# Attention: one half gate chunk of each unit moves from ahead of the first turn of the probabilities to behind the last one

## The chip, the cores and the metric

One core of a Trainium2 chip runs the whole program. The metric is device time in microseconds (us), as the median of several executions. The profile comes from one more execution. The engines are called PE (TensorE matmuls), PEld (TensorE weight loads), DVE (VectorE), ACT (ScalarE), POOL (GpSimd) and SP (SyncE, which only issues DMAs here).

## The reference, cut to what matters

The program computes two blocks, one after the other. The second block has two layers, and each begins with a projection, sliding window attention with 16 meta tokens, and a convolution branch. What matters here is, for each layer:

```
u = h @ w_in[i]                      # q, k, v, conv inputs and two gates come out of one projection
s = q k^T * scale + bias             # per block of 128 queries: keys = 16 meta, 128 previous, 128 own
m = max(max(s), sink); p = exp(s - m); p = p / (sum(p) + exp(sink - m))
o = p_meta @ v_meta + p_band @ v_band
mix = (sigmoid(gate_a) * (o @ w_attn_proj) + sigmoid(gate_c) * y_conv) @ w_out
```

There are 8 query heads in 2 groups of 4 that share keys and values, and 512 tokens behind the 16 meta tokens. All is float32.

## The kernel before, in words

`project_and_attend` (L2351) does the projection and the attention of one layer. It is called once for each of the two layers. Its work on TensorE has two kinds.

The first kind is the projection. A *half chunk* is 128 output channels for 264 of the 528 token columns: 8 products over k, each of which the trace counts as 2 instructions (for float32 every matmul here is 2 instructions, the turns excepted). The accumulators are 2 PSUM banks, `ring`. ACT copies a bank out (`take`, L2560), and the half chunk after the next one needs that copy (`taken`, L2462). The last 32 half chunks are those of the gates (`gate`, L2470). They are needed only by the next stage, so 16 of them are kept for the attention, where they fill TensorE's time between the dependent steps. There they are issued in *parts*, each of 4 of the 8 products (8 instructions in the trace). The diff moves such parts: "a half gate chunk" in the title is such a part, half of a half chunk.

The second kind is the attention, in units. A unit is one block of queries with one group of heads. Layer 0 has 10 units: two for the meta queries, with one block of keys, two with two blocks of keys (the first real block has no previous one), and six with three. Layer 1 has 8: two with two blocks, six with three. For unit u the steps are:

- `scores(u + 1)` on TensorE (L2484), one unit ahead;
- `turn(u, m)` on TensorE (L2500), one for each block m of keys: four transposes of the probabilities into the PSUM bank `ptr`. The turn of m = 0 waits for `scaled` of the unit (POOL, L2456). Each turn waits for `t_out` of the one before, since there is one bank;
- the move of `ptr` to `pt` on ACT (L2624), one for each turn, which raises `t_out`;
- `weigh_values(u)` on TensorE (L2510), the products with the values, which waits for the last `t_out`.

On DVE, behind `scores(u + 1)`: the bias, the maximum, and at the end `maxed` (L2694). On ACT, behind the move of m = 0: `soft(u + 1)` (L2569), four exponentials with sums and a small one, which waits for `maxed`. Then DVE inverts the sum (L2698) and POOL scales the probabilities. ACT closes the unit by copying the result out (L2629, `o_out`). Behind unit `len(units) - 4` ACT also runs four Silus over the convolution's result (L2634).

How many parts a unit gets is set by `upto(u)` (L2409), which spreads the 16 half chunks evenly: in layer 0 the ten units get 2, 4, 2, 4, 4, 2, 4, 2, 4, 4 parts, in layer 1 every unit gets 4. Before the change the unit's parts stand as follows (numbers of parts in brackets, for 3 blocks and 4 parts): scores(u+1), [2], turn 0, [1], turn 1, [1], turn 2, weigh_values(u). With 3 blocks and 2 parts it is scores, turn 0, [1], turn 1, [1], turn 2, weigh_values. ACT has the same order written out: it takes those half chunks that are complete by then, ahead of the move of each turn.

```
stop = last_part - (len(keys) - 1 - m)           # PE, L2549: parts up to here stand ahead of turn m
stop = (last_part - (len(keys) - 1 - m)) // 2    # ACT, L2617: half chunks taken ahead of move m
```

Of the kernel before, what the change touches and what calls it, by code (L numbers as in the profile page):

```python
# [2350 lines left out]
def project_and_attend(core, A, i, weights, mix_in):  # L2351
# [5 lines left out]
    for n in range(TILES):  # L2357
        for hk in range(KVH):
            keys = [(0, META, TILES)] + ([(META + (n - 1) * P, P, n - 1)] if n else []) + [(META + n * P, P, n)]
# [10 lines left out]
    with ExitStack() as ctx:  # L2370
# [38 lines left out]
        def upto(u):  # L2409

            return EARLY + 2 + (GATES - EARLY - 2) * (u + 1) // len(units)

        def slot(j):

            return j % 2 * 2 + j // 2
# [10 lines left out]
        with core.block() as block:  # L2426
# [32 lines left out]
            def _(pe):  # L2459
# [24 lines left out]
                def scores(u):  # L2484
                    hk, nq, q0, keys = units[u]
                    if u:
                        pe.wait_ge(s_read, u)
                    lo, width = keys[-1][0] + keys[-1][1], sum(k[1] for k in keys[1:])
                    for j in range(G):
                        c, b = divmod(j, 2)  # L2490
                        rows = slice(b * HD, (b + 1) * HD)
                        q = core.q_t[rows, hk * 2 + c, q0:q0 + nq]
                        last = pe.matmul(meta(u)[:, b, c, :], q, core.k_t[rows, hk, 0:META], start=True, stop=True)
                        if width:
                            last = pe.matmul(main(u)[:, b, c, 2 * P - width:], q, core.k_t[rows, hk, lo - width:lo], start=True, stop=True)
                    last.then_inc(s_made, 1)
# [3 lines left out]
                def turn(u, m):  # L2500
                    hk, nq, q0, keys = units[u]
                    at, nk = sum(k[1] for k in keys[:m]), keys[m][1]
                    if moves[0]:
                        pe.wait_ge(t_out, moves[0])
                    for j in range(G):
                        last = pe.transpose(ptr[0:nk, j * nq:(j + 1) * nq], s[0:nq, u % 2, slot(j), at:at + nk], ident[0:nq, 0:nq])
                    last.then_inc(t_made, 1)
                    moves[0] += 1

                def weigh_values(u):  # L2510
                    hk, nq, q0, keys = units[u]
                    pe.wait_ge(t_out, moves[0])
                    if u:
                        pe.wait_ge(o_out, u)
                    for m, (k0, nk, vt) in enumerate(keys):
                        for par in range(2):
                            heads = pt[0:nk, m, 0:G * nq].rearrange("p (c r q) -> p c r q", r=2, q=nq)[:, :, par, :]
                            last = pe.matmul(po[par * HD:(par + 1) * HD, 0:2 * nq], core.v_tok[0:nk, vt, hk * HD:(hk + 1) * HD],
                                             heads, start=m == 0, stop=m == len(keys) - 1)
                    last.then_inc(o_made, 1)  # L2520
# [22 lines left out]
                done = 2 * (EARLY + 2)  # L2543
                for u, (hk, nq, q0, keys) in enumerate(units):
                    if u + 1 < len(units):
                        scores(u + 1)
                    last_part = 2 * upto(u)
                    for m in range(len(keys)):
                        stop = last_part - (len(keys) - 1 - m)  # L2549
                        for part in range(done, stop):  # L2550
                            gate(part // 2, part % 2)
                        done = max(done, stop)
                        if m == 0:
                            pe.wait_ge(scaled, u + 1)
                        turn(u, m)
                    weigh_values(u)

            @block.scalar
            def _(act):
                def take(n, dst, f, half):  # L2560
                    act.wait_ge(projected, n + 1)
                    act.activation(dst[:, cols(half)], ring[:, n % RINGS, 0:HALF], f).then_inc(taken, 1)

                def gate(h):
                    if h // 2 >= 2 * DK - CCK - 1:
                        act.wait_ge(normed, CCK)
                    take(gate_half(h), core.gates[:, h // 2, :], ACT.Copy, h % 2)

                def soft(u):  # L2569
                    hk, nq, q0, keys = units[u]  # L2570
                    width = sum(k[1] for k in keys)
                    x = st[0:nq, u % 2]
                    act.wait_ge(maxed, u + 1)
                    for j in range(G):
                        act.activation(s[0:nq, u % 2, j, 0:width], s[0:nq, u % 2, j, 0:width], ACT.Exp,
                                       bias=x[:, 2, j:j + 1], accum_out=x[:, 3, j:j + 1])
                    act.activation(x[:, 1, :], x[:, 1, :], ACT.Exp).then_inc(exped, 1)

                act.wait_ge(padded, 1)
                for n in range(first_gate):  # L2580
                    c, half = divmod(n, 2)
                    if c < 4:
                        take(n, val[:, c, :], ACT.Copy, half)
                    elif c < 8:
                        take(n, glu[:, c - 4, CW - 1:], ACT.Sigmoid, half)
                    elif c < 12:
                        take(n, core.q_t[:, c - 8, :], ACT.Copy, half)
                    else:
                        take(n, core.k_t[:, c - 12, :], ACT.Copy, half)
                act.wait_ge(v_made, 1)  # L2590
                act.activation(core.v_tok[:, 0:4, :].rearrange("p t c -> p (t c)"), ps[:, 0, :], ACT.Copy)
                act.activation(core.v_tok[0:META, 4, :], ps[0:META, 1, 0:P], ACT.Copy).then_inc(v_out, 1)
                for h in range(EARLY):
                    gate(h)
                act.wait_ge(centred, CCK)
                act.wait_ge(taken, SUMS)
                act.sem_inc(taken, 1)
                for c in range(CCK):
                    act.wait_ge(centred, CCK + c + 1)
                    if c == CCK - 1:  # L2600
                        act.wait_ge(taken, SUMS + 1)
                        act.sem_inc(taken, 1)
                    act.activation(sq[:, c, :], core.conv[:, c, :], ACT.Square).then_inc(squared, 1)
                for h in range(EARLY, EARLY + 2):
                    gate(h)
                for half in range(2):
                    n = SQUARES + half
                    act.wait_ge(projected, n + 1)
                    act.activation(rt[:, cols(half)], ring[:, n % RINGS, 0:HALF], ACT.Sqrt, scale=1.0 / CC, bias=eps).then_inc(taken, 1)
                act.wait_ge(taken, SQUARES + 2)  # L2610
                act.sem_inc(rooted, 1)
                soft(0)
                moves, done = 0, EARLY + 2
                for u, (hk, nq, q0, keys) in enumerate(units):
                    last_part = 2 * upto(u)
                    for m, (k0, nk, _) in enumerate(keys):
                        stop = (last_part - (len(keys) - 1 - m)) // 2  # L2617
                        for h in range(done, stop):
                            gate(h)
                        done = max(done, stop)  # L2620
                        act.wait_ge(t_made, moves + 1)
                        if u:
                            act.wait_ge(o_made, u)
                        act.activation(pt[0:nk, m, 0:G * nq], ptr[0:nk, 0:G * nq], ACT.Copy).then_inc(t_out, 1)  # L2624
                        moves += 1
                        if m == 0 and u + 1 < len(units):
                            soft(u + 1)
                    act.wait_ge(o_made, u + 1)
                    act.activation(core.attn[:, hk * 2:hk * 2 + 2, q0:q0 + nq],  # L2629
                                   po[:, 0:2 * nq].rearrange("p (c q) -> p c q", c=2), ACT.Copy).then_inc(o_out, 1)  # L2630
                    if u == len(units) - 4:
                        for c in range(CCK):
                            act.wait_ge(normed, c + 1)
                            act.activation(core.conv[:, c, :], core.conv[:, c, :], ACT.Silu, scale=param(c, 0), bias=param(c, 1)  # L2634
                                           ).then_inc(silu, 1)
# [967 lines left out]
```

## Time and profile before

| | |
|---|---|
| Time, median of 3 runs | 3231.21 us (3228.75 to 3231.43) |
| The profiled execution's own time | 3231.08 us |
| Its span | 3229.2 us |
| TensorE busy (matmuls) | 93% of the span |
| DVE, ACT, POOL busy | 32%, 17%, 7% |
| Attention units of layer 0 | about 1373 to 1492 us |
| Attention units of layer 1 | about 2292 to 2404 us |

A row of the timeline gives start, duration, engine, line, operation, output and inputs, and how many instructions were merged. Behind it, in brackets, stands how long the engine had been idle and what ended that idle time; "issue" means nothing that the profile shows. PE and PEld are the same queue: a load stands ahead of its matmul. Starts of loads are the better clock for TensorE's order, since they show when the queue reached a step.

### The profile page before, as it was taken

The page shows a single profiled execution, that of the slowest core. Times are in us where ns is not written, and L with a number is a line of the kernel's source. Part 1 is how long each engine was busy: PE and PEld are TensorE (multiplying, and loading weights), DVE is VectorE, ACT ScalarE, POOL GpSimd, SP SyncE. Part 2 cuts the span into 40 slices and gives each one's busy share as a digit, 9 for nine tenths or more (in the row PEclk, how much of TensorE's full clock was granted, in tenths as well). Part 3 has the DMA queues.
Part 4 walks back from the last instruction along what each step waited for, and adds up shares of the span by engine and source line. Part 5 has one row for each costly group of instructions (what it writes and reads, how often), then busy time and mean ns, then how long its engine had stood idle before and what let it go on. Part 6 is the DMA issues. An engine that isn't in the chain of part 4 may idle for free. (4 is left out here: it accounts for less than half of the span.)

```text
span 3229.2 us, 43786 instructions
## 1 busy us (share of the span) xinstructions
PE 2990.9 (93%) x18418; PEld 1848.2 (57%) x18418; DVE 1048.4 (32%) x1946; ACT 548.7 (17%) x1262; POOL 220.9 (7%) x204
## 2 busy tenths in 40 slices
PE   8998899999789979989999999999999799999897
PEld 4544787654343338867578884478776444444343
DVE  5666665553311234631300002119212311010004
ACT  3222333221111121133000000011240000000001
POOL 0001321340000000011000000000010100000000
PEclk9999899999889989999999999999999799999998
DMA  3411000115389921202012142012120615547917
GB/s 115 107 52 43 4 16 29 40 48 237 139 340 430 418 89 70 86 21 118 0 52 78 68 166 78 0 68 74 61 81 13 248 50 223 215 171 322 417 48 292
DMA packets 79477, 414.03 MB, mean 128 GB/s; under 512 B 10675, under 2 KB 16179, under 8 KB 63588
## 3 DMA queue, kind: packets, MB, share of 16 engines
q1 hardware_dynamic: 68028, 384.75, 30.0%
q10 hardware_dynamic: 7848, 14.61, 1.8%
q0 software_dynamic: 3456, 12.58, 1.1%
q8 instruction: 109, 1.79, 0.2%
q14 instruction: 36, 0.29, 0.0%
HBM read 383.17 MB, written 28.76 MB: 128 GB/s over the span
## 5 line engine op out<-in xcount | busy, mean ns | idle before, releaser
L3312 PE MATMUL pgu<-gu,xg 128*64 128x320 f32 (+1 forms) x2560 | 393.5, 463 | 8.9 <-POOLq L3240 8.9
L2887 PE MATMUL pp<-feat,lead 128*128 128x264 f32 x1408 | 315.9, 388 | 2.0 <-DVEq L2901 2.0
L3312 PEld LDWEIGHTS pgu<-gu,xg 128*64 128x64 f32 x2560 | 182.3, 137 | 204.8 <-issue 130.4
L2887 PEld LDWEIGHTS pp<-feat,lead 128*128 128x128 f32 x1408 | 269.1, 191 | 48.6 <-DVEq L2901 2.2
L312 PE MATMUL proj<-feat,w 128*128 128x512 f32 x576 | 256.0, 598 | 2.6 <-PEq L153 2.6
L2465 PE MATMUL ring<-feat,lead 128*128 128x264 f32 x1024 | 244.6, 400 | 3.0 <-PEq L2912 1.5
L2465 PEld LDWEIGHTS ring<-feat,lead 128*128 128x128 f32 x1024 | 200.6, 198 | 42.6 <-issue 7.0
L3319 PE MATMUL py<-down,hm_t 128*64 128x512 f32 x880 | 200.3, 603 | 10.5 <-POOLq L3240 10.5
L2465 PE MATMUL ring<-feat,w 128*128 128x264 f32 x896 | 208.1, 390 | 0.0
L2465 PEld LDWEIGHTS ring<-feat,w 128*128 128x128 f32 x896 | 169.8, 192 | 31.5 <-issue 3.1
L312 PEld LDWEIGHTS proj<-feat,w 128*128 128x128 f32 x576 | 107.4, 191 | 124.8 <-issue 124.8
L497 DVE SCALAR_TENSOR_TENSOR mixed<-padded,taps,mixed 128x512 f32<-128x512 f32 x216 | 162.4, 752 | 7.7
L2657 DVE SCALAR_TENSOR_TENSOR conv<-vg,cols,conv x240 | 163.4, 764 | 0.0
L2932 PE MATMUL po<-wd,hm 128*128 128x512 f32 x352 | 151.9, 593 | 0.0
L3319 PEld LDWEIGHTS py<-down,hm_t 128*64 128x64 f32 x880 | 62.0, 139 | 121.9 <-issue 104.5
L3381 DVE TENSOR_TENSOR hm<-sg,pgu 128x384 f32<-128x384 f32 (+1 forms) x40 | 20.9, 521 | 316.7 <-PE pgu L3312 209.2
L2905 DVE TENSOR_TENSOR hm<-gb,pp 128x528 f32 x22 | 15.5, 704 | 305.1 <-ACT gb L2897 305.1
L2932 PEld LDWEIGHTS po<-wd,hm 128*128 128x128 f32 x352 | 66.6, 190 | 83.2 <-issue 83.1
L2772 PE MATMUL pp<-wo,feat 128*128 128x512 f32 x256 | 111.3, 593 | 2.8 <-POOL feat L2821 2.8
L3264 ACT ACT_TABLE_LOAD x19 | 24.4, 1283 | 461.1 <-PE pgu L3312 280.7
L2772 PEld LDWEIGHTS pp<-wo,feat 128*128 128x128 f32 x256 | 48.1, 190 | 61.9 <-issue 61.9
L2219 ACT ACTIVATE rt<-rt 128x1 f32<-128x1 f32 (+1 forms) x15 | 3.0, 203 | 379.7 <-DVE rt L2189 379.7
(493 smaller groups left out, 3488.1 us busy)
## 6 DMA issues: line engine op xcount, KB each, us to landing
gu<-in_moe_gu SPq DMA_DIRECT2D x16, 3072.0 KB, 10.0
gu<-in_moe_gu SPq DMA_DIRECT2D x16, 2560.0 KB, 15.7
ring<-in_w_gate SPq DMA_DIRECT2D x16, 2048.0 KB, 13.3
ring<-in_w_up SPq DMA_DIRECT2D x16, 2048.0 KB, 15.0
ring<-in_w_down SPq DMA_DIRECT2D x16, 2048.0 KB, 17.2
w<-in_w_in SPq DMA_DIRECT2D x15, 2048.0 KB, 7.8
down<-in_moe_down SPq DMA_DIRECT2D x8, 3072.0 KB
lead<-in_ffn_up SPq DMA_DIRECT2D x22, 1024.0 KB, 4.8
```

Of the source, the lines that this page charges most:

```text
L312: last = pe.matmul(proj[:, n % 2, :], w[:, g % 2, k, c * P:(c + 1) * P], core.feat[:, k, :], start=k == 0, stop=k == DK - 1)
L497: dve.scalar_tensor_tensor(out=out, in0=src[:, j:j + SEQ], scalar=taps[:, n, j:j + 1], in1=out, op0=ALU.mult, op1=ALU.add).then_inc(convol ...
L2465: last = pe.matmul(ring[:, n % RINGS, 0:HALF], w[g % 2][:, c, k * P:(k + 1) * P], core.feat[:, k, cols(half)], start=k == 0, stop=k == DK - 1)
L2657: dve.scalar_tensor_tensor(out=out, in0=src[:, j:j + NTOK], scalar=tap(c, j), in1=out, op0=ALU.mult, op1=ALU.add).then_inc(own, 1)
L2772: last = pe.matmul(pp[:, n % 2, n // 2 % 2, 0, :], mixed[:, k, row_cols(t)], wo[:, k, half * BANK:(half + 1) * BANK], start=k == 0, stop=k ...
L2887: last = pe.matmul(pp[:, b, a, half, 0:HALF], w[:, b, a, k * P:(k + 1) * P], core.feat[:, k, half * HALF:(half + 1) * HALF], start=k == 0, ...
L2905: dve.tensor_tensor(halves(hm[:, bass.ds(r * 2 + b, 1), :].rearrange("p a n -> p (a n)")), halves(sg[:, b, :]), pp[:, b, 1, :, 0:HALF], AL ...
L2932: last = pe.matmul(po[:, n % TILES, :], hm[:, f, row_cols(t)], wd[:, half, f, :], start=f == 0, stop=f == FC - 1)
L3264: act.activation(sg[:, q, 0:n], pgu[:, 2 * q, 0:n], ACT.Silu).then_inc(silu, 1)
L3312: last = pe.matmul(pgu[half(h), part, 0:n], xg[:, k, :], w[:, k, h, :], start=k == 0, stop=k == DK - 1)
L3319: last = pe.matmul(py[half(h), :], hm_t[:, c, :], down[:, c, h * BANK:(h + 1) * BANK], start=c == 0, stop=c == XC - 1)
L3381: dve.tensor_tensor(hm[:, c0:c0 + n], sg[:, q, 0:n], pgu[:, 2 * q + 1, 0:n], ALU.mult).then_inc(multiplied, 1)
```

## The change

Every `stop` becomes one smaller, and what is left of the unit's parts stands behind the last turn, ahead of `weigh_values`. On ACT the half chunk that is complete only by then is taken behind the last move. With 3 blocks and 4 parts the order on TensorE becomes scores, [1], turn 0, [1], turn 1, [1], turn 2, [1], weigh_values; with 3 blocks and 2 parts scores, turn 0, turn 1, [1], turn 2, [1], weigh_values; with 2 blocks and 4 parts scores, [2], turn 0, [1], turn 1, [1], weigh_values; with 1 block one part of the bulk goes behind the turn. ACT's order for 3 blocks and 4 parts was take, move 0, soft, move 1, take, move 2. It becomes move 0, soft, take, move 1, move 2, take.

```diff
                     last_part = 2 * upto(u)
                     for m in range(len(keys)):
-                        stop = last_part - (len(keys) - 1 - m)
+                        stop = last_part - (len(keys) - m)
                         for part in range(done, stop):
                             gate(part // 2, part % 2)
                         done = max(done, stop)
                         if m == 0:
                             pe.wait_ge(scaled, u + 1)
                         turn(u, m)
+                    for part in range(done, last_part):
+                        gate(part // 2, part % 2)
+                    done = max(done, last_part)
                     weigh_values(u)
...
                     for m, (k0, nk, _) in enumerate(keys):
-                        stop = (last_part - (len(keys) - 1 - m)) // 2
+                        stop = (last_part - (len(keys) - m)) // 2
                         for h in range(done, stop):
                             gate(h)
                         done = max(done, stop)
...
                             soft(u + 1)
+                    for h in range(done, last_part // 2):
+                        gate(h)
+                    done = max(done, last_part // 2)
                     act.wait_ge(o_made, u + 1)
```

## Rows read from the trace of the kernel before

**Rows 1.** The page: busy time, share of the span, instructions of TensorE.
```profile
PE 2990.9 (93%) x18418; PEld 1848.2 (57%) x18418; DVE 1048.4 (32%) x1946; ACT 548.7 (17%) x1262; POOL 220.9 (7%) x204
```

**Rows 2.** Groups by line, of `weigh_values`: busy, mean ns | idle before, releaser.
```profile
L2518 PE MATMUL po<-pt,v_tok 128*64 128x256 f32 (+2 forms) x184 | 27.7, 416 | 17.8 <-ACT pt L2624 17.8
L2518 PEld LDWEIGHTS po<-pt,v_tok 128*64 128x64 f32 (+1 forms) x184 | 10.6, 139 | 30.3 <-ACT pt L2624 21.8 <-issue 6.9
```

**Rows 3.** Timeline of layer 1, unit 3: three blocks of keys, four parts.
```profile
2352.48 3.41 PEld L2465 LDWEIGHTS ring<-feat,w 128*128 128x128 f32 x16 [0.33 <-issue]
...
2355.58 0.16 DVE L2694 TENSOR_SCALAR st<-st 128x4 f32<-128x4 f32 x1
2355.93 0.53 PEld L2506 LDWEIGHTS ptr<-cst,s 128*16 128x16 f32 x4
...
2357.28 0.50 ACT L2575 ACTIVATE s<-s,st 128x272 f32<-128x272 f32 x1
...
2358.15 0.58 PEld L2506 LDWEIGHTS ptr<-cst,s 128*128 128x128 f32 x4
...
2358.70 1.64 PEld L2465 LDWEIGHTS ring<-feat,w 128*128 128x128 f32 x8
...
2359.40 0.57 ACT L2624 ACTIVATE pt<-ptr 128x512 f32<-128x512 f32 x1
...
2360.37 0.58 PEld L2506 LDWEIGHTS ptr<-cst,s 128*128 128x128 f32 x4
...
2361.22 0.60 ACT L2624 ACTIVATE pt<-ptr 128x512 f32<-128x512 f32 x1
2361.87 0.19 PEld L2518 LDWEIGHTS po<-pt,v_tok 16*64 16x64 f32 x4 [0.92 <-ACT pt L2624]
```

**Rows 4.** Timeline of layer 0, units 1 and 2: small loads and a first turn behind parts.
```profile
1394.61 0.14 PEld L2506 LDWEIGHTS ptr<-cst,s 16*16 16x16 f32 x4 [0.34 <-issue]
...
1398.57 0.32 PEld L2506 LDWEIGHTS ptr<-cst,s 128*16 128x16 f32 x4 [0.27 <-POOL s L2456]
```

**Rows 5.** Timeline of layer 0, unit 3: two blocks of keys, the last turn.
```profile
1412.51 0.58 PEld L2506 LDWEIGHTS ptr<-cst,s 128*128 128x128 f32 x4
...
1413.75 0.36 ACT L2562 ACTIVATE gates<-ring 128x264 f32<-128x264 f32 x1
...
1414.02 0.57 ACT L2624 ACTIVATE pt<-ptr 128x512 f32<-128x512 f32 x1
...
1414.64 0.19 PEld L2518 LDWEIGHTS po<-pt,v_tok 16*64 16x64 f32 x4 [1.56 <-ACT pt L2624]
```

**Rows 6.** Timeline of TensorE's loads, layer 0, units 5 and 7 (two parts).
```profile
1437.70 0.42 PEld L2506 LDWEIGHTS ptr<-cst,s 128*128 128x128 f32 x4 [1.85 <-ACT pt L2624]
1439.05 0.19 PEld L2518 LDWEIGHTS po<-pt,v_tok 16*64 16x64 f32 x4 [0.92 <-ACT pt L2624]
...
1458.56 0.42 PEld L2506 LDWEIGHTS ptr<-cst,s 128*128 128x128 f32 x4 [1.74 <-ACT pt L2624]
1458.94 1.64 PEld L2465 LDWEIGHTS ring<-feat,w 128*128 128x128 f32 x8
```

**Rows 7.** Timeline of layer 1, unit 5, whose exponentials stand behind the Silus.
```profile
2374.04 0.42 PEld L2506 LDWEIGHTS ptr<-cst,s 128*128 128x128 f32 x4 [1.11 <-ACT pt L2624]
```

**Rows 8.** Timeline of both layers' first units, where DVE is late.
```profile
1382.75 0.51 PEld L2493 LDWEIGHTS pm<-k_t,q_t 64*128 64x128 f32 x4 [4.94 <-DVE s L2679]
...
2304.18 0.41 ACT L2575 ACTIVATE s<-s,st 128x144 f32<-128x144 f32 x1 [4.29 <-DVE st L2694]
...
2306.78 0.29 PEld L2518 LDWEIGHTS po<-pt,v_tok 16*64 16x64 f32 x4 [5.54 <-ACT pt L2624]
```

**Rows 9.** Timeline of the matmuls, layer 0: two parts twice, and the scores ahead.
```profile
1416.70 1.09 PE L2495 MATMUL ps<-k_t,q_t 64*128 64x256 f32 x4
1417.72 5.17 PE L2465 MATMUL ring<-feat,lead 128*128 128x264 f32 x16
...
1441.54 0.79 PE L2495 MATMUL ps<-k_t,q_t 64*128 64x256 f32 x4
1442.25 3.83 PE L2465 MATMUL ring<-feat,w 128*128 128x264 f32 x16
```

**Rows 10.** Windows of 4 us: time, busy of each engine, PEclk, DMA.
```profile
1416.00:1420.00 4.00, 4.00 (x21) 2.89 (x20) 2.14 (x3) 0.31 (x1) 0.33 (x1) 0.63 0.00 0
...
2324.00:2328.00 4.00, 4.00 (x22) 2.95 (x21) 1.62 (x3) 0.38 (x1) 0.57 (x1) 0.63 0.00 0
```

**Rows 11.** Timeline of SP where the next stage begins, layer 1.
```profile
2404.61 0.37 SPq L2739 DMA_DIRECT2D late<-in_w_mix  x1
```

## The prediction

> **What bounds the kernel now.** I read the page first. TensorE's matmuls are busy for 93% of the span and no other engine passes 32% [rows 1], so a stretch gets shorter only if TensorE stands still less in it. The groups by line then say where it stands still in the attention: the products with the values were held back for 17.8 us by ACT's move of the turned probabilities, over both layers (21.8 us counted at their loads) [rows 2]. That is the whole prize of this kind, 0.6% of the span. It can't all be won, since that idle time includes waits that have other causes. The timeline shows what ends it, unit by unit. In a unit with three blocks of keys the last turn's loads start at 2360.37, ACT's move runs from 2361.22 to 2361.82, and the values' first load starts at 2361.87 [rows 3]. Turn, move and products are a chain with nothing of TensorE's beside it.
>
> **What a moved part covers.** All distances are from load to load. Two parts ahead of the first turn take 2355.93 - 2352.48 = 3.45, so 1.72 each. A turn takes 2358.70 - 2358.15 = 0.55 of the queue, the part behind it 2360.37 - 2358.70 = 1.67. From the last turn to the products it is 2361.87 - 2360.37 = 1.50 [rows 3]. The part behind the last turn thus reaches 0.55 + 1.67 = 2.22 and hides the move, with 0.7 to spare.
>
> What the trace of before does not show is a values' load directly behind a part. Its first block is 16 rows by 64 columns. The nearest row is the 16 by 16 load of a meta unit's turn behind parts, idle 0.34 under "issue" [rows 4]. From below the cost is 0, as for the 128-row loads of a turn behind a part, which show no idle time [rows 3]. From above it is the 0.34 of that row. I take 0.34, as the shape is the nearer one.
>
> The Trainium skill (TensorE: Matmul & The Clock Gate, Part 2, step-by-step) says that TensorE's queue pulls a weight load ahead of matmuls in flight when the row groups don't conflict or when it goes to the background buffer. By it the 0.34 would be 0, for 17 units 5.8 us more. The row speaks against it for small loads; it is a rival below.
>
> **Units with three blocks and four parts** (layer 0: 4, 6, 8; layer 1: 2, 3, 4, 6; seven in all). Before, the part ahead and the chain cost 1.72 + 1.50 = 3.22; after, 0.55 + 1.67 + 0.34 = 2.56. That is -0.66. But the first turn now comes 1.72 sooner, and ACT has a half chunk to take between the exponentials and the second move. Count from the first part: `maxed` is done at 2355.74 - 2352.48 = 3.26. The exponentials, which before began when the first move let them, now wait for it and begin at 3.29. They take 2359.40 - 2357.28 = 2.12 [rows 3], the take 1414.02 - 1413.75 = 0.27, the move 0.57 [rows 5], and the load follows 0.05 later: 6.30. The third turn would be there at 1.72 + 2 x 2.22 = 6.16. So there is a new stall of 0.14, and the unit gives -0.52. Seven: -3.6.
>
> **The last unit of each layer** has no exponentials between its moves: -0.66 each, -1.3.
>
> **Two blocks and four parts** (layer 0: 3; layer 1: 1). Before, 1414.64 - 1412.51 = 2.13 from last turn to products, since the move stands behind exponentials and a take [rows 5]. With the part ahead 3.85. After, 2.56: the part covers them, and the take stands behind the move. -1.3 each, -2.6.
>
> **Layer 0, unit 2** (two blocks, two parts): its first turn already waited 0.27 for POOL [rows 4], and now no part stands ahead of it. Between 0 and -1.3, I take -0.8.
>
> **The meta units.** Unit 0's slack is swallowed: scores(2) wait for DVE until 1382.75 whatever TensorE does before [rows 8]. Unit 1 gives a little, -0.3 (0 to -0.6). **Layer 1, unit 0**: DVE is late, the exponentials begin at 2304.18 for lack of a maximum, and the products follow at 2306.78 [rows 8]. Only the 0.27 of the take that no longer stands ahead of the second move is won: -0.3.
>
> **Where it costs.** Units 5 and 7 of layer 0 get only two parts. No part stands ahead of their first turn before or after, so the one put behind the last turn comes from between turns 0 and 1, where it had covered the first move. The third turn was already waiting for the second move (1.85 idle in unit 5), and goes on waiting to the same moment. Behind it stood 1439.05 - 1437.70 = 1.35; now 0.38 (turn after a wait, 1458.94 - 1458.56) + 1.67 + 0.34 = 2.39 [rows 6]. +1.05 each, +2.1. In unit 5 of layer 1 the exponentials follow the Silus and the third turn waits 1.11 [rows 7]. The same loss of 1.05, less what the earlier first turn gives, since the table load and exponentials behind it start sooner: between -0.5 and +1.05, I take +0.2.
>
> **Sum of the waits:** -3.6 - 1.3 - 2.6 - 0.8 - 0.3 - 0.3 + 2.1 + 0.2 = -6.6 us. No DMA moves: all loads that SP issues in this stage wait for half chunks up to the sixteenth, which lie ahead of the units. The next stage's loads are issued on its entry, 2404.61 [rows 11], and move forward with it. ACT's takes are as many as before, and it is far from full (17%) [rows 1].
>
> **The clock.** Behind the wait of 1.56 in unit 3 of layer 0 [rows 5] the granted clock stands at 0.63 over 4 us, a mean of the levels of 2.4 and 1.2 GHz. The same happens behind the like unit of layer 1 [rows 10]. The price: scores 1.09 against 0.79, two parts 5.17 against 3.83 [rows 9], so 1.6 each time. Afterwards these two units have no wait but the 0.34. I take both falls as gone: -3.3 (0 to -3.3). The long idle stretches of the first units and of those with the Silus stay, so I leave their falls as they are.
>
> The Trainium skill (the same page, Part 1, "What's actually happening") says that the full clock is not the default but is released by recent activity. It would speak against units 5 and 7: there the idle time gathers in longer pieces. The trace agrees in the sense that falls stand behind idle stretches.
>
> Forecast: -6.6 - 3.3 = -9.9. The sum is made against the profiled execution's 3231.08 (span 3229.2, 1.9 around it), 0.13 below the median. So 3231.2 - 9.9 = 3221.3.
>
> **The rivals, and how the numbers follow.** A measurement of this kernel tells about 0.2% from no change, 6.5 us: faster is below 3224.7.
> - The forecast, chance 0.50: 3221.3, its own range 3218.5 to 3224.
> - Waits alone, 0.20: the clock still falls as often, or in other places. 3224.6. If unit 5 of layer 0, whose idle stretches grow to about 1 and 2.4 us, falls as well, add up to 3.2 (two of the 1.6): 3227.8. For it: the falls depend on where an idle stretch lies, as unit 2 had a similar wait and no fall. Half of this case is still faster by 0.2%.
> - Loads pulled ahead, 0.14: the values' first loads overlap the part, as those of 128-row turns do. -9.9 - 17 x 0.34 = -15.7: 3215.5. For it: rows of turns behind parts; against: the 0.34.
> - Given back, 0.11: the time won returns in a later wait for data that doesn't move with the stage. 3231, at least 3226. Against: the DMA issues stand behind the stage's end.
> - ACT becomes the bound, 0.05, slower: the take ahead of the second move and the later start of the exponentials hold the third turn in the seven four-part units and two-part ones. A unit loses once that stall passes 0.66 instead of my 0.14. At 1.9, if the exponentials ran as late against the turn as in the Silu units, seven units give 7 x (1.9 - 0.66) = +8.7 in place of -3.6: -6.6 + 12.3 = +5.7, and with falls of the clock behind those stalls (two of 1.6) +8.9: 3240. Against: `maxed` at 3.26 is read, not guessed.
>
> Faster 0.47 + 0.10 + 0.14 = 0.71, within 0.2% 0.24, slower 0.05. The range 3215 to 3228 leaves out the last two cases and little else.
>
> **What would show it.** The idle time of the values' products for ACT's move falls from 17.8 to nearly 0, with about 0.34 under "issue" at their loads. The third turn of the four-part units shows a wait of about 0.1 to 0.2 for ACT. Units 5 and 7 of layer 0 show a new wait at turn 1 and are about 1 us longer. The clock stays at 1.0 behind the two-block units. The prediction is wrong if the values' load waits for more than 0.34, or if the slow clock turns up behind units that had none.

## The result and the profile after

The changed kernel takes 3211.78 us (median of 6 runs, 3207.07 to 3214.02) against 3231.61 for the kernel before (6 runs, 3228.75 to 3236.62). The ratio is 0.9934, with a 95% interval of 0.9924 to 0.9944. A second measurement on another chip gave 0.9932 (0.9918 to 0.9946). The forecast was 3221.3 with a range of 3215 to 3228: the direction was right, the gain of 19.8 us is twice the 9.9 that I forecast, and the time lies below the range.

In the rows, L2565, L2578, L2627 and L2700 are the lines that were L2562, L2575, L2624 and L2694 before.

The page, and the groups of the values' products and of the turns after the change (compare [rows 1, 2]):

```profile
PE 2981.5 (93%) x18418; PEld 1840.9 (57%) x18418; DVE 1047.9 (33%) x1946; ACT 549.4 (17%) x1262; POOL 220.6 (7%) x204
```

```profile
L2518 PE MATMUL po<-pt,v_tok 128*64 128x256 f32 (+2 forms) x184 | 26.4, 400 | 4.4 <-ACT pt L2627 4.4
L2518 PEld LDWEIGHTS po<-pt,v_tok 128*64 128x64 f32 (+1 forms) x184 | 10.3, 136 | 18.9 <-issue 12.0 <-ACT pt L2627 5.2
L2506 PE MATMUL ptr<-cst,s 128*128 128x128 f32 (+2 forms) x184 | 28.2, 276 | 10.5 <-ACT pt L2627 7.9 <-POOL s L2456 2.6
```

The values' products waited 17.8 for ACT's move, and now 4.4, nearly all of it in the first unit of layer 1. Part of that went to the turns, as the sum had said: they waited 5.2 before and 10.5 now. The turns before:

```profile
L2506 PE MATMUL ptr<-cst,s 128*128 128x128 f32 (+2 forms) x184 | 27.1, 269 | 5.2 <-ACT pt L2624 5.0
```

But look at the busy column too: TensorE's matmuls were busy for 2990.9 and are busy for 2981.5 with the same 18418 instructions. Over the two attentions alone (the first number behind the comma is the busy time of the matmuls, in brackets their number) before and after are:

```profile
1372.90:1493.16 120.26, 103.17 (x585) 76.77 (x584) 32.02 (x78) 47.66 (x149) 14.87 (x10) 0.91 0.03 13
2292.02:2404.63 112.61, 100.41 (x545) 74.95 (x545) 28.81 (x63) 44.79 (x127) 14.30 (x8) 0.91 0.03 13
```

```profile
1370.71:1482.88 112.17, 99.65 (x585) 73.47 (x585) 32.12 (x78) 48.35 (x149) 14.85 (x10) 0.95 0.04 14
2279.59:2382.48 102.89, 95.76 (x545) 70.92 (x544) 28.80 (x63) 44.89 (x127) 14.29 (x8) 0.95 0.04 14
```

That is 8.2 us less busy time for the same matmuls, and the granted clock (the number behind the busy times of the five engines) is 0.95 on average instead of 0.91. The removal of waits doesn't shorten busy time. Instructions ran faster. (The other 1.2 of the 9.4 lie outside the attention, where busy time varies from trace to trace.)

A four-part unit of layer 1 after the change (unit 4; compare unit 3 in [rows 3]):

```profile
2335.65 1.63 PEld L2465 LDWEIGHTS ring<-feat,w 128*128 128x128 f32 x8 [0.33 <-issue]
2337.32 0.53 PEld L2506 LDWEIGHTS ptr<-cst,s 128*16 128x16 f32 x4
...
2338.75 0.16 DVE L2700 TENSOR_SCALAR st<-st 128x4 f32<-128x4 f32 x1
2338.94 0.52 ACT L2578 ACTIVATE s<-s,st 128x272 f32<-128x272 f32 x1 [0.18 <-DVE st L2700]
...
2341.07 0.37 ACT L2565 ACTIVATE gates<-ring 128x264 f32<-128x264 f32 x1
2341.34 0.58 ACT L2627 ACTIVATE pt<-ptr 128x512 f32<-128x512 f32 x1
2341.97 0.42 PEld L2506 LDWEIGHTS ptr<-cst,s 128*128 128x128 f32 x4 [0.25 <-ACT pt L2627]
2342.36 1.64 PEld L2465 LDWEIGHTS ring<-feat,w 128*128 128x128 f32 x8
2342.67 0.60 ACT L2627 ACTIVATE pt<-ptr 128x512 f32<-128x512 f32 x1 [0.74 <-PE ptr L2506]
2344.34 0.19 PEld L2518 LDWEIGHTS po<-pt,v_tok 16*64 16x64 f32 x4 [0.34 <-issue]
```

The move (2342.67 to 2343.27) lies under the part (2342.36 to 2344.00). The values' load waits 0.34 under "issue", and the third turn has its new wait, 0.25. The unit takes 11.90 instead of 12.60.

The time of the attention tells how the gain is divided. All times in this table and the next are from load to load. I count the attention from the first load of scores(1) to the first load of the next stage's products. What lies outside is the rest of the span. The distances between the values' products of neighbouring units give the share of each unit.

| us | layer 0 | layer 1 | rest of the span |
|---|---|---|---|
| before | 120.26 | 112.61 | 2996.3 |
| after | 112.17 | 102.89 | 2991.6 |
| difference | -8.1 | -9.7 | -4.7 |

The rest is not touched by the change. Over the fourteen traces of this study it lies anywhere between 2990.4 and 3000.1, with no relation to the edit that I can see, so I take its 4.7 here as scatter. The attention is worth 17.8.

From here on, *slow clock* is time in which TensorE's granted clock is 1.2 GHz and not 2.4, and a *fall* is one stretch of it. In layer 1 the units behave very unequally. Units 3, 4 and 7 got 0.7 to 0.75 shorter each, unit 5 stayed within 0.1, but unit 2 got 2.33 shorter and unit 6 3.94. In layer 0 unit 8 got 3.93 shorter. In the trace before, a fall stands behind the values of the unit ahead of each of these three, and in the trace after it is absent. Windows of 4 us show it. Before, layer 1, behind unit 5:

```profile
2376.00:2380.00 4.00, 4.00 (x25) 2.80 (x24) 0.00 (x0) 0.39 (x1) 0.00 (x0) 0.53 0.00 0
2380.00:2384.00 4.00, 4.00 (x14) 2.71 (x12) 3.05 (x6) 0.00 (x0) 0.00 (x0) 0.62 0.00 0
```

After, the same place:

```profile
2356.00:2360.00 4.00, 4.00 (x28) 2.55 (x28) 0.00 (x0) 1.36 (x3) 1.23 (x1) 1.00 0.00 0
2360.00:2364.00 4.00, 4.00 (x27) 3.14 (x26) 2.70 (x4) 0.37 (x2) 0.00 (x0) 1.00 0.00 0
```

The granted clock is 0.53 and 0.62 before, 1.00 after. The clock no longer falls to 1.2 GHz behind the unit whose exponentials follow the Silus, although that unit waits just as long in all: one wait of 1.93 (loads) for ACT instead of 1.11 and 0.92. What differs is where it waits. Before, wait, turn, wait, small products and small scores followed one another, some 7 us (2373.4 to 2380.7) with no gate part among them. Now the part stands between. That this is the cause is not shown by these two traces; the experiments below test it.

Added up over the windows, the clock was at 1.2 GHz for 20.5 us in layer 0 and 20.4 in layer 1 before, and for 10.2 in each after. In layer 1 what is left stands behind the first unit, as before. In layer 0 three short falls are left: behind the first unit, in unit 5, which had none before, and in unit 7.

### The profile page after: what moved, and what is told of

It is laid out like the page before. It is cut to its first block and busy times, and to the rows that moved or that the text cites. A ratio compares the mean times of both kernels' runs of the same rounds, so it can differ in the third digit from the quotient of the medians.

```text
span 3206.7 us, 43786 instructions
## 1 busy us (share of the span) xinstructions
PE 2981.5 (93%) x18418; PEld 1840.9 (57%) x18418; DVE 1047.9 (33%) x1946; ACT 549.4 (17%) x1262; POOL 220.6 (7%) x204
```

## The experiments

**Theory (clock).** The waits give about 8 us. Another 10 come from falls of the clock that no longer occur, since the part puts full products (128 rows by 128 columns) into the long stretch between the last gate part and the next one. **Rival (waits).** The hidden waits alone gave it, and I mis-sized them. **Second rival (elsewhere).** The excess arises outside the attention.

In the next table the layers, the rest of the span and the time at 1.2 GHz (layer 0 + layer 1) come from one profiled execution each, and the ratios from timed runs.

| label | layer 0 | layer 1 | rest | at 1.2 GHz | ratio to before (95%) |
|---|---|---|---|---|---|
| before | 120.26 | 112.61 | 2996.3 | 20.5 + 20.4 | |
| e12_before_again | 123.40 | 112.62 | 3000.1 | 27.3 + 20.4 | one execution |
| changed | 112.17 | 102.89 | 2991.6 | 10.2 + 10.2 | 0.9934 (0.9924 to 0.9944) |
| e5_changed_again | 112.09 | 102.94 | 2998.7 | 10.3 + 10.2 | 0.9932 (0.9918 to 0.9946) |
| e1_layer1 | 123.39 | 102.82 | 2996.3 | 27.3 + 10.2 | 0.9966 (0.9952 to 0.9979) |
| e2_filler | 114.87 | 107.75 | 2998.7 | 3.4 + 6.8 | 0.9966 (0.9954 to 0.9978) |
| e11_filler_all | 113.29 | 104.63 | 2993.9 | 0 + 0 | 0.9946 (0.9929 to 0.9963) |
| e3_behind_values | 124.75 | 110.13 | 2993.2 | 20.5 + 6.9 | 1.0006 (0.9997 to 1.0015) |
| e4_short_units | 109.62 | 102.86 | 2990.4 | 10.2 + 10.2 | 0.9938 (0.9921 to 0.9955) |
| e6_fill_first | 112.04 | 98.85 | 2998.1 | 10.2 + 0 | 0.9917 (0.99 to 0.9933) |
| e7_spread | 104.07 | 97.67 | 2997.0 | 6.8 + 3.4 | 0.9911 (0.9893 to 0.9929) |
| e8_spread_fill | 101.76 | 96.08 | 2995.3 | 0 + 0 | 0.9882 (0.9867 to 0.9898) |
| e9_take_later | 112.01 | 102.33 | 2993.9 | 10.3 + 10.2 | one execution |
| e10_values_reversed | 112.18 | 102.93 | 2995.9 | 10.2 + 10.2 | one execution |

### The change in one layer

```diff
-    stop = last_part - (len(keys) - m)              # (and the same on ACT)
+    stop = last_part - (len(keys) - m - (1 - i))
```

> The change in layer 1 alone; layer 0 keeps the order of before. Read from the two traces, the attention of layer 1 got 9.7 us shorter and that of layer 0 8.1. If both stretches are independent of one another and the gain arises inside them, this kernel is 9 to 11 us faster than before (ratio 0.9966 to 0.9972). If the gain beyond my sum came from elsewhere (a part of the kernel that the change doesn't touch), it is nearer to 5, my forecast's share for that layer with the clock.

Measured: 3222.41, ratio 0.9966, 10.4 to 11 us faster. Layer 1 takes 102.82, as in the changed kernel, and the rest of the span 2996.3 as before. The gain arises inside the attention and is additive, so the second rival falls. Layer 0, in the order of before, took 123.39, not 120.26: its falls of the clock stood behind other units. That comes back below.

### Work in the wait, with no wait removed

```diff
                         turn(u, m)
+                    if u:
+                        pe.wait_ge(o_out, u)
+                    for e in range(2):
+                        pe.matmul(po[:, 0:256], ident, core.feat[:, e, 0:256], start=True, stop=True)
                     weigh_values(u)
```

> The order of before, and in each unit two additional products of 128x128 by 256 (results overwritten, 0.87 us) in TensorE's wait between the last turn and the values' products, where about 0.95 of the queue was idle. No wait of the attention gets shorter. Clock theory (the second half of the gain is slow clock that no longer occurs, since work of the full array now stands in the long stretch of turn, wait, small products and scores): the granted clock no longer falls behind most units, 4 to 8 us faster than before although the work grew. Waits theory (the gain is the hidden waits alone, mis-sized by me): 0 to 4 us slower than before, since each filler may delay the products by up to the 0.34 of a load behind a full product.

Measured: 3222.83, ratio 0.9966, 10 us faster than before, with more work and no wait taken away. The loads of TensorE in a four-part unit of layer 1:

```profile
2351.36 0.58 PEld L2506 LDWEIGHTS ptr<-cst,s 128*128 128x128 f32 x4
2351.91 0.73 PEld L2559 LDWEIGHTS po<-feat,cst 128*128 128x128 f32 x4
2352.97 0.19 PEld L2518 LDWEIGHTS po<-pt,v_tok 16*64 16x64 f32 x4 [0.33 <-ACT pt L2628]
```

From the turn to the values it is 1.61, against 1.50 before the filler: in each unit with three blocks ACT's move ends no sooner and the values start even 0.11 later (the unit takes 12.70 instead of 12.60). The two attentions take 5.4 and 4.9 less, with 3.4 + 6.8 us of slow clock instead of 20.5 + 20.4. All of the gain is clock. The windows behind unit 5 of layer 1, as above:

```profile
2365.00:2369.00 4.00, 3.86 (x31) 2.52 (x31) 0.01 (x1) 1.34 (x4) 2.00 (x1) 1.00 0.01 4
2369.00:2373.00 4.00, 4.00 (x24) 3.23 (x22) 2.99 (x6) 0.00 (x0) 0.00 (x0) 1.00 0.00 0
```

The waits rival expected 0 to 4 us slower. It falls, and the gain is larger than the 4 to 8 that the clock theory had given.

The Trainium skill (TensorE: Matmul & The Clock Gate, Part 1, "What's actually happening") says that the throttled clock is the default and that activity releases it. Before the runs I had used that only to fear for units 5 and 7. These runs agree with it in the direction that I had missed: added activity is worth time, even useless activity.

### The same with the first waits filled too, for the waits alone

Against the kernel of the last section:

```diff
-                    for e in range(2):
-                        pe.matmul(po[:, 0:256], ident, core.feat[:, e, 0:256], start=True, stop=True)
+                    for e in range(11 if u == 0 and i == 1 else 2):
+                        pe.matmul(po[:, 0:256], ident, core.feat[:, e % DK, 0:256], start=True, stop=True)
                     weigh_values(u)
+                    if u == 0 and i == 0:
+                        for e in range(8):
+                            pe.matmul(ptr[:, 0:256], ident, core.feat[:, e % DK, 0:256], start=True, stop=True)
```

> The order of before with the two additional products per unit, and also eight behind the first unit's products in layer 0 and nine more ahead of them in layer 1. Clock theory: no slow clock is left in layer 1 and little in layer 0, so its attention shows the waits alone. In layer 1 it should take 104 to 105 us, against 98.9 for the changed order with its first wait filled: the waits of the change are then worth 5 to 6 us there, and the rest of the 9.7 was clock. The whole kernel is 12 to 16 us faster than before. If the filler in the units did its work in another way than by the clock, filling the first waits changes nothing: 9 to 11 us faster, as without.

Measured: 3214.52, ratio 0.9946, 17.5 us faster than before and a little more than the 12 to 16 expected, and in layer 1 104.63, within the 104 to 105. The windows over both attentions show the full clock throughout:

```profile
1374.00:1487.00 113.00, 107.29 (x642) 80.95 (x640) 32.14 (x78) 47.44 (x148) 14.85 (x10) 1.00 0.04 14
2284.00:2389.00 105.00, 102.66 (x597) 78.60 (x595) 28.81 (x63) 44.75 (x126) 14.29 (x8) 1.00 0.04 16
```

The order of before without slow clock (104.63) against the changed order without slow clock (98.85, e6_fill_first below) gives the waits of layer 1: 5.8, of which about 0.7 are the fillers' own cost (0.11 in each of the six units with three blocks; with two blocks they cost nothing, 12.36 against 12.35 in unit 3 of layer 0). So the waits are worth 5.1 in layer 1, where the sum said 4.1, and the other 4.6 of its 9.7 are clock.

### Filling the first waits of the changed kernel

```diff
+                    if u == 0 and i == 1:
+                        for e in range(10):
+                            pe.matmul(po[:, 0:256], ident, core.feat[:, e % DK, 0:256], start=True, stop=True)
                     weigh_values(u)
+                    if u == 0 and i == 0:
+                        for e in range(5):
+                            pe.matmul(ptr[:, 0:256], ident, core.feat[:, e % DK, 0:256], start=True, stop=True)
```

> The changed kernel with additional 128x128 by 256 products (results overwritten) in the two longest waits: five behind the first unit's products in layer 0 (2.2 us of work in a wait of 3.3), ten ahead of the first unit's products in layer 1 (4.4 us in a wait of 4.8). No wait of the attention gets shorter. Clock theory: the slow clock behind them (about 10 us of it in each layer in three traces, so up to 5 us of time in all, part of it hidden in the wait) goes away, 3 to 5 us faster than the changed kernel, 23 to 25 faster than before. If only waits count: 0 to 1 us slower than the changed one.

Measured: 3209.79 (3203.34 to 3212.66), against 3213.31 (3210.68 to 3215.43) for the changed kernel on the same chip. The intervals of the two ratios overlap, so the medians alone don't settle it. The trace does for layer 1: 98.85 against 102.94, with no slow clock left over the whole attention of that layer, although the wait is there as before:

```profile
2295.48 4.30 PEld L2561 LDWEIGHTS po<-feat,cst 128*128 128x128 f32 x20
2300.26 0.19 PEld L2518 LDWEIGHTS po<-pt,v_tok 16*64 16x64 f32 x4 [0.49 <-ACT pt L2633]
```

```profile
2286.00:2385.00 99.00, 96.15 (x566) 72.49 (x565) 28.79 (x63) 45.12 (x127) 14.29 (x8) 1.00 0.04 14
```

In layer 0 unit 1 got 1.6 shorter, but the fall in unit 5 came at a worse place than in the changed kernel: units 5 and 6 took 12.67 + 14.04 instead of 13.17 + 11.89, 1.6 more. So that layer stayed at 112.04.

### The part one step further

```diff
+                    weigh_values(u)
                     for part in range(done, last_part):
                         gate(part // 2, part % 2)
                     done = max(done, last_part)
-                    weigh_values(u)
```

> The part goes one step further, behind the values' products and ahead of the next scores. The wait for ACT's last move stays as long as before, 0.92 at the loads. Clock theory: the stretch without full products is split all the same; the falls behind the four-part units go, some 5 us, against about 5 us that the new waits cost (0.15 at the third turn of seven units, and 1.7 in each of the two short units, whose part leaves a covered place): 0 to 3 us slower or faster than before. Waits theory: the 5 us of new waits stand alone, 4 to 7 us slower than before.

ACT's take stands behind its copy of the result accordingly. Measured: 3234.4, ratio 1.0006 (0.9997 to 1.0015), within the clock theory's 0 to 3 us and below the 4 to 7 of the rival (by the medians it is 1.6 slower). The loads of a four-part unit of layer 1:

```profile
2347.10 0.42 PEld L2506 LDWEIGHTS ptr<-cst,s 128*128 128x128 f32 x4 [0.25 <-ACT pt L2627]
2348.44 0.19 PEld L2518 LDWEIGHTS po<-pt,v_tok 16*64 16x64 f32 x4 [0.92 <-ACT pt L2627]
2349.02 0.63 PEld L2518 LDWEIGHTS po<-pt,v_tok 128*64 128x64 f32 x8 [0.39 <-issue]
2350.03 1.63 PEld L2465 LDWEIGHTS ring<-feat,lead 128*128 128x128 f32 x8 [0.38 <-issue]
```

The wait of 0.92 is as long as it was, and the unit takes 12.85 instead of 12.60. Still the layer is 2.5 shorter (110.13), with 6.9 us at 1.2 GHz instead of 20.4. A part behind the wait breaks the stretch as one inside it does. It is not that TensorE stands still for less time: its matmuls were idle for 14.2 us of layer 1 here (110.13 less 95.94 busy) and for 12.2 before. In layer 0 the two short units lose a covered place (units 5 and 7 take 12.57 and 15.10 instead of 10.60 and 12.28) and the clock falls there all the same, so the layer gets 4.5 longer and the gain is lost.

### The two short units in the order of before

```diff
+        def short(u):
+
+            parts = 2 * (upto(u) - (upto(u - 1) if u else EARLY + 2))
+            return 1 if parts < len(units[u][3]) else 0
...
-                        stop = last_part - (len(keys) - m)              # (and the same on ACT)
+                        stop = last_part - (len(keys) - m - short(u))
```

> The change, but the two units of layer 0 that have fewer parts than blocks of keys keep the order of before. By my sum the change costs 1.05 in each; in the trace after, unit 5 became 2.6 longer, 1.6 of it slow clock, and unit 7 1.2. If both the waits and the clock are as read, this kernel is 2 to 4 us faster than the changed one, 22 to 24 faster than before. If slow clock returns behind the longer stretch of these units (as before the change, behind unit 7), the clock part is lost and it is within 1 us of the changed one or slower by 1 to 2.

Measured: 3209.3 (5 runs, 3205.47 to 3219.66), ratio 0.9938 (0.9921 to 0.9955). By the times it can't be told from the changed kernel, and the expected 2 to 4 us are not confirmed. The trace shows the expected terms in place: layer 0 is 109.62 instead of 112.17, unit 5 takes 10.60 instead of 13.21, unit 7 12.28 instead of 13.46. No fall stood behind either unit in this trace. Against that, units 0 and 1 took 21.60 together instead of 20.34, with the first fall 10.2 us long instead of 3.4. It is shown for one execution, then, and for the median it stays open.

### Other numbers of parts, and that with filler

```diff
-            return EARLY + 2 + (GATES - EARLY - 2) * (u + 1) // len(units)
+            return EARLY + 2 + sum(((2, 1, 1, 1, 2, 2, 2, 2, 2, 1), (3, 2, 2, 2, 2, 2, 2, 1))[i][:u + 1])
```

> The changed order, and the 32 parts of each layer are spread otherwise: layer 0 gets 4, 2, 2, 2, 4, 4, 4, 4, 4, 2 and layer 1 gets 6, 4, 4, 4, 4, 4, 4, 2. No unit with exponentials between its moves and three blocks has fewer than four parts any more, and the first units' waits for DVE are filled with work that was to be done anyway. From the distances of the rows, step by step, layer 0 gets 7 us shorter than with the changed kernel and layer 1 2.5, before any effect of the clock: 9 to 12 us faster than the changed kernel, 28 to 32 faster than before. If time won here is given back behind the stage, nearer to the changed kernel.

Measured: 3203.47 (4 runs, 3200.73 to 3210.65), 9.8 us faster than the changed kernel, ratio to before 0.9911. Layer 0 is 8.0 shorter and layer 1 5.3. The sum of distances said 7 and 2.5. The rest is clock again, 10.2 us at 1.2 GHz instead of 20.5. (Together that is 13.3 in one trace of each, against 9.8 between the medians; the difference lies within the scatter of the rest.) One fall moved to unit 3 of layer 0, where the cut from four parts to two left a wait of 1.44:

```profile
1404.80 1.23 PE L2518 MATMUL po<-pt,v_tok 16*64 16x256 f32 x8 [1.44 <-ACT pt L2627]
...
1407.80 3.46 PE L2465 MATMUL ring<-feat,lead 128*128 128x264 f32 x8
```

A part there takes 3.46 instead of 1.95.

Against this kernel:

```diff
                     weigh_values(u)
+                    if u == 0 and i == 0:
+                        for e in range(3):
+                            pe.matmul(ptr[:, 0:256], ident, core.feat[:, e % DK, 0:256], start=True, stop=True)
```

and three more ahead of the first unit's products in layer 1, into `po`.

> The kernel with the parts spread otherwise, and three additional 128x128 by 256 products in each of the two first waits. Clock theory: the slow clock behind the first units shrinks further, 0 to 3 us faster than that kernel alone. If only waits count: the same or up to 1 us slower.

Measured: 3196.46 (4 runs, 3194.83 to 3196.76), ratio to before 0.9882 (0.9867 to 0.9898): 37 us faster than before and 17 faster than the changed kernel. It is the fastest version of this study. Against the kernel without filler it gained 7, more than the 0 to 3 expected. Of that the traces show 3.9 in the attention (2.3 in layer 0, 1.6 in layer 1); the rest lies within the scatter between executions, and the two intervals overlap a little. The granted clock is 1.00 over both attentions:

```profile
1374.00:1476.00 102.00, 96.31 (x592) 71.46 (x592) 32.11 (x78) 48.20 (x149) 14.86 (x10) 1.00 0.04 15
2273.00:2369.00 96.00, 92.85 (x550) 69.72 (x550) 28.78 (x63) 44.90 (x127) 14.29 (x8) 1.00 0.04 14
```

### Two single terms, one execution each

```diff
-                        stop = (last_part - (len(keys) - m)) // 2
+                        stop = (last_part - (len(keys) - m) - 1) // 2      # ACT only
```

> The changed kernel, but ACT takes the half chunk that stood between the exponentials and the second move behind that move. If the new wait of 0.25 at the third turn of the four-part units comes from this take (0.27) and not from the later start of the exponentials alone, the wait is gone and these units are 0.1 shorter (11.90 becomes 11.8), since a turn that doesn't wait takes 0.55 of the queue and one that waited 0.38. If it comes from the exponentials' wait for DVE, it stays.

Measured: 3210.88. The third turn no longer waits:

```profile
2339.92 1.64 PEld L2465 LDWEIGHTS ring<-feat,w 128*128 128x128 f32 x8
2341.59 0.58 PEld L2506 LDWEIGHTS ptr<-cst,s 128*128 128x128 f32 x4
2342.14 1.64 PEld L2465 LDWEIGHTS ring<-feat,w 128*128 128x128 f32 x8
```

The unit takes 11.84 instead of 11.90. The wait came from the take ahead of the move, as the sum said, and removing it is nearly worthless: a turn that waited takes 0.38 of the queue, one that didn't 0.55.

```diff
-                    for m, (k0, nk, vt) in enumerate(keys):
+                    for m, (k0, nk, vt) in reversed(list(enumerate(keys))):
...
-                                             heads, start=m == 0, stop=m == len(keys) - 1)
+                                             heads, start=m == len(keys) - 1, stop=m == 0)
```

> The changed kernel with the blocks of keys taken in reverse in the values' products, so that the first load behind the part has 128 rows by 64 columns instead of 16 by 64. If the 0.34 under issue comes from the small number of rows, it goes to 0 (the block of 16 rows may then wait behind the others); if it comes from the 64 columns or from changing to another shape at all, it stays at 0.34.

Measured: 3213.01. The first load behind the part now has 128 rows and still waits:

```profile
2348.54 0.63 PEld L2518 LDWEIGHTS po<-pt,v_tok 128*64 128x64 f32 x8 [0.34 <-issue]
2349.55 0.19 PEld L2518 LDWEIGHTS po<-pt,v_tok 16*64 16x64 f32 x4 [0.39 <-issue]
```

So the 0.34 is not a matter of few rows. It comes with the 64 columns or with the change of shape; these two were not told apart. The layer takes 102.93, as before the reversal, so the order costs nothing.

### A second trace of the kernel before

> The kernel before as it is, for a second trace of it. The falls of the clock behind the first units of both layers are there again; those behind the four-part units and the Silu units may stand behind other units of the same kind. The two attentions together take 230 to 238 us, against 232.9 in the first trace; what lies outside them is 2990 to 2999 us, as in all traces so far. If the falls of before are at fixed places, it is 232.9 within 0.5.

Measured: one execution of 3237.97. Layer 1 repeats to 0.01 (112.62), layer 0 takes 123.40 instead of 120.26. The falls of layer 0 moved: unit 3 is spared (unit 4 takes 12.16, not 13.81), and one now stands behind unit 5 (unit 6 takes 15.79, not 12.59), while that behind unit 7 costs more (17.24, not 15.84):

```profile
1440.00:1444.00 4.00, 2.98 (x16) 1.38 (x16) 0.18 (x1) 1.15 (x3) 2.00 (x1) 0.75 0.01 2
1444.00:1448.00 4.00, 4.00 (x21) 2.72 (x19) 0.51 (x2) 0.38 (x1) 0.00 (x0) 0.50 0.00 0
```

It is the same pattern as in the unchanged layer 0 of e1_layer1. The two traces of the changed kernel (after and e5_changed_again) have their falls in the same places, with every unit within 0.05. The attention of before is worth 232.9 or 236.0, that of the changed kernel 215.1 in both of its traces, so 17.8 to 21.0 lie between them, around the measured 19.8.

## Why the prediction was wrong, point by point

- **The mechanism of the waits was right, and its size nearly.** A part hides the move, the values' load waits 0.34 behind it, the third turn waits for ACT. Four-part units gave 0.70 each where no fall disturbs the reading, and the sum said 0.52; the last units gave 0.75 (0.66). The forecast wait of 0.14 was 0.25, but the turn behind a wait takes 0.38 of the queue, not 0.55. I had read that number and used it only for the short units. Over seven units that is 1.3 us.
- **Units with two blocks:** unit 3 of layer 0 gave 1.38 and unit 1 of layer 1 1.08, the forecast was 1.3 each. (In the second, the slow clock behind the first unit costs 0.3 more than before. Without slow clock it takes 12.36 in e11_filler_all and 10.97 in e6_fill_first, 1.39 less.) Unit 2 of layer 0 gave 0.78 (0.8).
- **The short units** lost as forecast: unit 7 of layer 0 1.18 and unit 5 2.61 (1.05 each). Of the 2.61, 1.6 are a fall of the clock that I had named as a rival: in e9_take_later that fall is absent and unit 5 takes 11.62, 1.02 more than before. Unit 5 of layer 1 stayed as it was (+0.07 against +0.2). The first unit of layer 1 gave 0.29 (0.3). The meta units gave 0.3 (0.3): without slow clock the values of the second start 19.61 behind the first load of scores(1) in e11_filler_all and 18.74 in e6_fill_first, and 0.61 of the first is filler (1.25 from turn to values instead of 0.64).
- **All waits together** come to about 8.2 (17.8 less the 9.6 of clock read below), the sum said 6.6. The turn behind a wait, 1.3, is nearly all of the difference.
- **The step that failed** is in "The clock": "The long idle stretches of the first units and of those with the Silus stay, so I leave their falls as they are." The waits stayed, as said. The falls did not. Between the two traces the clock gave back 1.65 behind unit 3 and 3.23 behind unit 7 of layer 0, 1.75 around unit 1 of layer 0 (its values start at 22.35 before and 20.34 after, and without slow clock and filler at 19.00 and 18.74), 1.63 and 3.24 behind units 1 and 5 of layer 1, less 1.59 in unit 5 of layer 0 and 0.31 in unit 1 of layer 1. That is 9.6, where my term for the clock was 3.3: I had counted only those behind unit 3 and unit 1. I took a fall for the price of an idle stretch that stays as long as it was. The filler shows that the fall can go while the chain that TensorE waits for stays: with two products in each wait, slow clock went from 20.5 + 20.4 to 3.4 + 6.8 us and the kernel gained 10. The filler also shortens the idle time in the wait (0.92 becomes 0.33 at the values' loads), but the part behind the values leaves it at 0.92, and slow clock went from 20.4 to 6.9 in layer 1 all the same. So the idle time alone doesn't decide it: where the full products stand counts too. Whether the small products in the stretch count for the clock as idle time does is not shown: no run varied them alone.
- **The prediction's own signs.** The values' products still wait 4.4, in the first unit of layer 1, whose wait the sum had itself left standing. One sign of being wrong came true: slow clock turned up behind a unit that had none, unit 5 of layer 0.
- **Rivals:** the loads are not pulled ahead (0.34 stays, in both orders of the blocks). Nothing was given back behind the stage. ACT did not become the bound: the third turn waits 0.25, and a unit would lose from 0.66 on. Of the second rival, the waits alone, the fall in unit 5 of layer 0 came true in both traces of the changed kernel; the 1.6 that it cost are in the 9.6 above.

## What to carry to other kernels

Where TensorE alternates between full products, waits and small products, look at the granted clock behind each such stretch before pricing an edit, and price the edit by what it puts into the stretch, not only by the wait that it hides: here a movable piece of full work was worth slightly more for the clock (9.6) than for the wait (8.2). In this kernel it helped inside a long run of waits and small products or right behind one (layer 1 of e3_behind_values), and where a unit gave up two of its four parts, a fall came back (unit 3 of e7_spread). More than that about the best place was not tested. A trace of one execution shows only one arrangement of the falls, so take two of the kernel before.

## What I had not expected of the hardware

Additional products with no use made the kernel 10 us faster (0.9966). The fastest version has the parts spread otherwise and six such products, 12 more matmul instructions and as many loads than the changed one, and is 17 us faster; about 10 of that came with the spreading alone. Falls of the clock also move between executions of the same program: layer 0 of the kernel before took 120.26 in one trace and 123.40 in another with the same waits.
